# A residual's scale and shift, moved from between the state-space steps to behind them

## The reference, cut to what matters

```
# norm behind the first FFN (layer 0)
x = layer_norm(ALPHA * x + f, ln2_g[0], ln2_b[0])

# odd mixer (layer 1)
z, xbc, dt_raw, pool_in = split(x @ w_in)
xbc = silu(causal_dwconv(xbc, conv_w, conv_b)); xs, bm, cm = split(xbc)
y = ssd_chunked(xh * dt, dt * a, bm, cm) + d_skip * xh       # state-space part
y = rms_norm(y * silu(z), ssm_norm)
p = multiscale_pool(pool_in, ...)
y = concat([y, p]) @ w_out

x = layer_norm(ALPHA * x + y, ln1_g[1], ln1_b[1])
...
def layer_norm(x, g, b):
    return (x - mean) * rsqrt(var + eps) * g + b
```

## Time and profile before

| | |
|---|---|
| Median of 3 runs | 2135.18 us (2133.06 to 2135.19) |
| The profiled execution | 2134.34 us, its span 2132.5 us |
| TensorE busy (matmuls) | 2106.9 us, 99% of the span |
| VectorE busy | 1273.1 us, 60% |
| ScalarE busy | 922.4 us, 43% |
| GpSimd busy | 123.5 us, 6% |
| Granted TensorE clock, mean | 0.998 |

### The profile page before, as it was taken

The page is one execution under the profiler, slowest core; times in us unless marked ns, Lnnn a source line. Parts: engine busy times, 40 slices in busy tenths (PEclk is TensorE's granted clock), DMA queues, the critical chain, the costliest instruction groups (busy, mean ns, idle before and its releaser), DMA issues.

```text
span 2132.5 us, 26271 instructions
## 1 busy us (share of the span) xinstructions
PE 2106.9 (99%) x10388; PEld 1713.6 (80%) x10388; DVE 1273.1 (60%) x1968; ACT 922.4 (43%) x1549; POOL 123.5 (6%) x170
## 2 busy tenths in 40 slices
PE   9999999999999999999999999999999999999998
PEld 7866688888888758888888878887788878888887
DVE  7445575555437876755553648665678756555534
ACT  4135553333425465433342543264555745333421
POOL 0000031000000001400000000000132500000000
PEclk9999999999999999999999999999999999999999
DMA  5312123333332212333323322312432023333332
GB/s 205 98 60 79 60 90 99 99 99 112 96 99 90 79 41 99 100 99 99 118 93 96 116 93 80 99 40 70 146 121 89 21 80 114 94 98 99 119 93 75
DMA packets 54649, 200.32 MB, mean 94 GB/s; under 512 B 6072, under 2 KB 6136, under 8 KB 53504
## 3 DMA queue, kind: packets, MB, share of 16 engines
q1 hardware_dynamic: 54528, 198.65, 28.6%
HBM read 194.38 MB, written 4.24 MB: 93 GB/s over the span
## 4 chain that ended last, share of the span: by engine, by line
PE 91%; DVE 4%; ACT 3%; DMA 1%; issue 1%; SPq 0%; ACTq 0%; DVEq 0%
PE bank L487 27%; PE bank L489 27%; PE bank L488 27%; PE bank L1053 2%; PE bank L776 1%; PE bank L757 1%; ACT arena L1349 1%; DMA ring<-stream 1%; DVE small L2045 1%; PE bank L793 1%; PE bank L704 1%; DVE xs L2040 0%; ACT whi L1244 0%; PE bank L848 0%; PE bank L1023 0%
## 5 line engine op out<-in xcount | busy, mean ns | idle before, releaser
L487 PE MATMUL bank<-xs,whi 128*128 128x512 f32 (+2 forms) x1992 | 769.9, 386 | 6.3 <-DVE xs L2040 2.9
L489 PE MATMUL bank<-xs,wlo 128*128 128x512 f32 (+2 forms) x1992 | 750.2, 377 | 0.0
L488 PE MATMUL bank<-xs,whi 128*128 128x512 f32 (+2 forms) x1992 | 749.7, 376 | 0.0
L2019 DVE TENSOR_TENSOR wlo<-ring,whi 128x1024 fp32r<-128x1024 f32 x333 | 416.6, 1252 | 290.5 <-ACT whi L1244 290.2
L1244 ACT ACTIVATE whi<-ring 128x1024 fp32r<-128x1024 f32 x333 | 350.3, 1053 | 259.8 <-DMA ring<-stream 259.5
L487 PEld LDWEIGHTS bank<-xs,whi 128*128 128x128 f32 x1992 | 375.3, 188 | 90.9 <-issue 12.5
L489 PEld LDWEIGHTS bank<-xs,wlo 128*128 128x128 f32 x1992 | 375.1, 188 | 69.2
L488 PEld LDWEIGHTS bank<-xs,whi 128*128 128x128 f32 x1992 | 375.6, 189 | 67.0 <-issue 2.9
L487 PE MATMUL bank<-whi,xs 128*128 128x512 f32 (+1 forms) x808 | 314.6, 389 | 0.7 <-issue 0.7
L489 PE MATMUL bank<-whi,xs 128*128 128x512 f32 (+1 forms) x808 | 311.4, 385 | 0.0
L488 PE MATMUL bank<-wlo,xs 128*128 128x512 f32 (+1 forms) x808 | 311.4, 385 | 0.0
(11 more groups left out here) (377 smaller groups left out, 1716.4 us busy)
## 6 DMA issues: line engine op xcount, KB each, us to landing
ring<-stream SPq DMA_DIRECT2D x333, 512.0 KB, 3.5
arena<-gains SPq DMA_DIRECT2D x5, 1024.0 KB, 5.5
arena<-gate_rows SPq DMA_DIRECT2D x16, 256.0 KB, 3.9
arena<-xt SPq DMA_DIRECT2D x4, 512.0 KB, 6.1
arena<-xn SPq DMA_DIRECT2D x1, 2048.0 KB, 7.8
kept<-arena SPq DMA_DIRECT2D x1, 2048.0 KB, 7.2
arena<-factor_rows SPq DMA_DIRECT2D x8, 256.0 KB, 4.8
arena<-kept SPq DMA_DIRECT2D x1, 2048.0 KB, 7.8
```

Of the source, the lines that this page charges most:

```text
L487: nc.tensor.matmul(out, ah, bh, start=first, stop=False)
L488: nc.tensor.matmul(out, ah, bl, start=False, stop=False)
L489: return nc.tensor.matmul(out, al, bh, start=False, stop=last)
L2019: V.tensor_tensor(wlo[:, v % SLOTS, :], ring[:, v % SLOTS, :], whi[:, v % SLOTS, :], ALU.subtract).then_inc(wlo_done, 1)
```

## The change

The table `residual_at` and its branch in the loop of the steps are gone. The eight operations, and the two waits ahead of them, now stand in VectorE's order behind the four `operand_low` and ahead of `token_norm`, first the four multiplications and then the four additions. Each addition waits for its tile's multiplication as before. No other engine's program is changed, and no operation is added or left out.

```diff
-        residual_at = {2 + 3 * x: divmod(x, 2) for x in range(2 * TILES)}
...
                     if n - 1 in out1_splits:
                         split_units(out1_splits[n - 1])
-                    if n in residual_at:
-                        tt, x = residual_at[n]
-                        if n == 2:
-                            dve.wait_ge(gb_sem, 16 * 2)
-                            dve.wait_ge(tensor_out, tensor_at.find("turned", "ln2_0", TILES - 1, 1))
-                        if x:
-                            dve.wait_ge(vector_out, vector_at.find("scaled", tt))
-                            V.tensor_tensor(XT[:, tt, :], XT[:, tt, :], GB[:, 1, :], ALU.add).then_inc(vector_out, vector_at.next("res", "ln2_0"))
-                        else:
-                            V.tensor_tensor(XT[:, tt, :], XT[:, tt, :], GB[:, 0, :], ALU.mult).then_inc(vector_out, vector_at.next("scaled", tt))
...
                 for k in range(4):
                     operand_low(k)
+                dve.wait_ge(gb_sem, 16 * 2)
+                dve.wait_ge(tensor_out, tensor_at.find("turned", "ln2_0", TILES - 1, 1))
+                for tt in range(TILES):
+                    V.tensor_tensor(XT[:, tt, :], XT[:, tt, :], GB[:, 0, :], ALU.mult).then_inc(vector_out, vector_at.next("scaled", tt))
+                for tt in range(TILES):
+                    dve.wait_ge(vector_out, vector_at.find("scaled", tt))
+                    V.tensor_tensor(XT[:, tt, :], XT[:, tt, :], GB[:, 1, :], ALU.add).then_inc(vector_out, vector_at.next("res", "ln2_0"))
                 token_norm("out1", "ln1_1", ALPHA, "layer", lambda: dve.wait_ge(vector_out, vector_at.find("res", "ln2_0")))
```

## The result

The changed kernel takes 2137.94 us (median of 19 runs, 2135.71 to 2139.6) beside 2134.24 us (19 runs, 2131.73 to 2136.52) for the kernel before: a ratio of 1.0019, with a 95% interval of 1.0013 to 1.0025, or 2.8 to 5.3 us slower. The forecast was 4.7 us slower.

What follows compares the result with a forecast made beforehand. TensorE, busy for 99% of the span, was taken as the bound. Steps 0, wait 3.3 and clock 1.4 gave +4.7 us: 2134.34 to 2139.0, plus 0.84 for the median, forecast 2139.9 us, range 2136.5 to 2142.4.

Steps and rivals of the forecast that it cites:

- Nothing is gained in the steps: State-space steps: removing the eight operations gains between 0 and 1.8 us of TensorE's time; 0 was taken.
- The test by the idle times of VectorE and ScalarE: Steps' end: idle times of 0.84 and 2.52 us show both queues empty after the last of the eight.
- 9.1 us of queue, 3.6 covered: VectorE ahead of the norm: the eight need 9.1 us, of which 3.6 us fall in its idle time.
- TensorE stops at unit 6 for 2.72 us, at unit 7 for 0.34: Output products: TensorE waits for VectorE's late weight splits, 2.72 us before unit 6 and another 0.34 before unit 7.
- The wait's price of 3.3 us: Output products: the waits and a slow first matmul make the second sum 3.3 us late; bounds 0 and 9.1.
- VectorE's own queue adds nothing: Norm: VectorE finishes the first sum and its moments by 827.9, before the second sum at 829.1, adding 0 us.
- The clock, 1.4 us: Behind TensorE's new pause: the granted clock falls to its lower level, costing 1.4 us; bounds 0 and 1.7.
- rival A: Behind TensorE's new pause: the clock holds, only the wait is paid, +3.3 us, 2138.5 us; chance 0.24.
- The second sum at 829.1: Norm: the second sum, at 825.83 before, comes at 829.1 us.
- Nothing takes it up later: Norm and FFN behind the second sum: no later idle time absorbs the delay, including TensorE's 1.57 us at 852.67.
- The time itself, 2139.9 us: Whole kernel: forecast 2139.9 us, 0.22% slower; chance 0.60.
- the forecast's own: Whole kernel: range 2138.2 to 2141.6 us, from a clock loss of 0 to 1.7 us and the runs' scatter.

Runs made afterwards that it cites:

- none: The eight operations left out of the changed kernel altogether: 2134.0 us, ratio 1.0002 to the kernel before.
- look_after: The changed kernel profiled once more without edit: 2138.64 us in one run, from the operand operations to the next FFN's first convolution 3.30 us longer than before.
- fill: The changed kernel with TensorE multiplying units 4 and 5 of three further half tiles ahead of unit 6: ratio 1.0005 to the kernel before.
- splits_between: The changed kernel with the splits of out1's units 6 and 7 taken behind three and five of the eight operations: ratio 1.0013 to the kernel before.
- twelve: The changed kernel with four more operations of the same shape behind the eight: ratio 1.0038 to the kernel before.

## Why the prediction was right

- *Nothing is gained in the steps.* Right but for 0.1 us (42.20 us of TensorE's time with the eight, 42.11 without): `none` takes as long as before, and the drained end keeps its waits of 1.46 and 0.65 us. The test by the idle times of VectorE and ScalarE behind the last of the eight, 0.84 and 2.52 us, carried it. With the eight gone ScalarE's waits for the gate fell from 4.3 to 2.9 us, and TensorE had no more than that 0.1 us of it.
- *9.1 us of queue, 3.6 covered.* Right. The eight took 810.79 to 819.95, 9.16 us.
- *TensorE stops at unit 6 for 2.72 us, at unit 7 for 0.34.* Right in place and nearly in size. By starts, unit 6 would have begun at 817.78 + 0.68 = 818.46 and began at 821.14, 2.68 us late; the profile counts 2.52 and 0.17 us of idle time, since it ends a matmul some 0.16 us after the next could start (2.68 less 2.52).
- *The wait's price of 3.3 us.* Right to the tenth: 3.30 in `look_after`, where there is nothing beside it.
- *VectorE's own queue adds nothing.* Right for the change, and only just: without TensorE's wait the queue alone costs 1.9 to 2.1 us, by `fill` and `splits_between`.
- *The clock, 1.4 us.* The price is right (4.73 to 4.87 less 3.30 is 1.4 to 1.6), the certainty is not. The prediction argued that a pause longer than two that brought a fall brings one too; what it had was one execution, in which both places happened to fall. The same pauses go without a fall in 5 and in 4 of 14 profiles. The forecast and rival A are one kernel in two executions, three profiles of four on the forecast's side; that the first profile had the fall, and so came within 0.2 us of the sum, is luck in part. Weighted so, the cost is by my estimate 3.3 + 0.75 x 1.5 = 4.4 us; the ratios give 4.1 and 4.7. The page of the Trainium skill that was weighed there (TensorE: Matmul & The Clock Gate, section "HAM oscillation — how this bites in real kernels") tells of a kernel in which each pause brings the fall; its waits are given as some 3 to 5 us. It does not carry over to a pause of 2.5 us: here the fall is chance for pauses of this length, while for the 7.06 us of `twelve` the one profile had it. Its way of counting the loss gives 0.84 + 0.84 = 1.7 us for the two stretches from 820 to 828 us, of which 1.4 to 1.6 reach the end of the way.
- *The second sum at 829.1.* By the times of the two profiles it came only 1.77 us later than before (827.60, was 825.83). Counted from the moment at which unit 6 is due it came 4.86 us later: before 825.83 - 821.55 = 4.28 us behind it, now 827.60 - 818.46 = 9.14. Read straight from the two pages, the loss would have looked like 2 us.
- *Nothing takes it up later.* Right: from the first convolution to the end of the span it is 1275.7 us before and 1275.9 after.
- *The time itself, 2139.9 us.* The median of 2137.94 lies 1.9 us below it, inside the wide range of 2136.5 to 2142.4 and just below the forecast's own of 2138.2 to 2141.6. Of the 1.9 us, 0.9 is that the three runs of before which the forecast started from stood high (2135.18; 19 runs gave 2134.24). What holds is the difference and its parts, not the absolute time.

## What to carry to other kernels

Moved work costs what it delays the first result that the bound engine asks for, not its length and not its stage: here four of the operations were free, eight cost 3.3 to 4.9 us, and the same eight were free again one wait earlier. So look in the order of time for the idle stretch that holds the whole of it, and check what stands right behind it in the queue. A cost of a few microseconds can't be read from the spans of two profiles where the clock falls by chance; measure from an instruction ahead of the edit to one behind it, and time the whole in many rounds.

## What was not expected of the hardware

The same program with the same pauses gets a fall of the clock in some executions and not in others, at three places, and a fall is worth 1.4 to 1.7 us in most cases and about twice that in three of the 14 profiles (0.68 in `look_after` above is one of them). The scatter of a kernel's runs goes with it. These are 75 runs of the kernel before, sorted by their mean granted clock:

| mean clock | runs | mean time, us |
|---|---|---|
| 1.000 | 1 | 2130.35 |
| 0.999 | 28 | 2131.45 |
| 0.998 | 31 | 2133.55 |
| 0.997 | 15 | 2135.44 |

A step of 0.001 of some 2132 us is 2.1 us of clock lost, and the means of the three large groups rise by 2.1 and 1.9: the scatter is lost clock. The falls at the two places that every kernel has are of this size, so they are likely to make up most of it; where the runs that were not profiled lost theirs is not shown. It also accounts for the profiled pair: the kernel before had both falls ahead of the change's place, the changed one had neither, and at L2318 (now L2307) it was 3.09 us ahead. Of these, 1.41 are there by the first wait of the steps (744.32 and 742.91), 0.09 are the steps, and 1.59 come between the drained end's last wait and L2318 (23.96 and 22.37 us). 4.87 - 3.09 and 0.2 behind give the 2.0 us between the spans. The Trainium skill (TensorE: Matmul & The Clock Gate, section "What's actually happening") calls the number of slow matmuls at a kernel's start variable between runs; the same is seen here in the middle of one.
